# A transformer pair on one core: the first third rebuilt, with unnormed token-major products first and the depthwise convolution spread

## The reference, cut to what matters

```python
xn = rms_norm(h, norm1_g)                      # per token, then a gain per feature
proj = xn @ w_in                               # 1024 x 5136
sg_u, sg_v, g_q, g_k, g_v, g_r, g_a, a_q, a_k, a_v, c_a, c_g = split(proj)
y_a = gelu(sg_u) * (W_s layer_norm(gelu(sg_v)) + b)         # spatial gating, 128-token blocks
y_b = gated_linear_attention(g_q, g_k, g_v, g_r, g_a)       # 4 heads, chunks of 64
y_c = band_chunk_attention(a_q, a_k, a_v)                   # 8 heads, softmax
y_d = silu(layer_norm(causal_dwconv31(c_a * sigmoid(c_g))))  # 31 taps per channel
for n, y in enumerate((y_a, y_b, y_c, y_d)):
    merged += sigmoid(xn @ w_gate[n] + b_gate[n]) * (y @ w_branch[n])
h = h + merged @ w_out
h = h + relu(rms_norm(h) @ w_ff1)**2 @ w_ff2
h = h + sigmoid(rms_norm(h) @ w_ple_gate + b) * (p @ w_ple);  h = rms_norm(h)
```

## Time and profile before

| | us |
|---|---|
| three runs | 980.77, 983.38, 982.29; median 982.29 |
| the profiled execution | 980.21, of which the span 978.9 |
| TensorE busy, weight loads busy | 924.2, 892.8 |
| VectorE, ScalarE, GpSimd busy | 745.7, 551.5, 1.9 |
| HBM read | 186.53 MB, 192 GB/s over the span |

### The profile page before, as it was taken

One profiled execution on the slowest core, in us unless ns is written; L12 is line 12 of the kernel. 1 busy time (PEld: TensorE's weight loads), 2 busy tenths in 40 slices (PEclk: granted clock), 3 DMA queues, 4 the chain that ended last, 5 costly groups with the idle time before them and its releaser, 6 DMA issues.

```text
span 978.9 us, 18386 instructions
## 1 busy us (share of the span) xinstructions
PE 924.2 (94%) x7342; PEld 892.8 (91%) x7342; DVE 745.7 (76%) x1199; ACT 551.5 (56%) x789; POOL 1.9 (0%) x9
## 2 busy tenths in 40 slices
PE   5999998999999999999999779999999989999995
PEld 5998987899999999999999779989989989999995
DVE  6899989677566799988887789987667885555543
ACT  6565445667644676654444458658584564444442
POOL 0000000000000000000000000000000000000000
PEclk9999999999999999999999999999999999999998
DMA  6765534454464699988883345445344545555541
GB/s 241 230 186 207 162 126 151 130 194 149 154 208 134 211 346 331 393 315 319 314 301 115 111 158 172 151 148 157 128 132 154 187 154 193 196 196 192 183 141 44
DMA packets 52820, 188.77 MB, mean 193 GB/s; under 512 B 6000, under 2 KB 6784, under 8 KB 52608
## 3 DMA queue, kind: packets, MB, share of 16 engines
q1 hardware_dynamic: 52736, 187.60, 56.9%
HBM read 186.53 MB, written 1.05 MB: 192 GB/s over the span
## 4 chain that ended last, share of the span: by engine, by line
PE 64%; DVE 24%; ACT 7%; issue 4%; DMA 1%; SPq 0%; DVEq 0%; ACTq 0%
PE bank L867 20%; PE bank L870 19%; PE bank L869 19%; DVE wlo L900 8%; DVE cv L973 3%; ACT whi L1679 1%; DVE mqk L1250 1%; DVE nrm L915 1%; DVE scr L1084 1%; DVE t L948 1%; DVE Alo L941 1%; ACT L1687 0%; DMA araw<-in_ada 0%; DMA raw<-in_stream 0%; PE bank L608 0%
## 5 line engine op out<-in xcount | busy, mean ns | idle before, releaser
L900 DVE TENSOR_TENSOR wlo<-raw,whi 128x1024 fp32r<-128x1024 f32 x297 | 358.1, 1221 | 56.9 <-ACT whi L1679 56.4
L867 PE MATMUL bank<-Alo,whi 128*128 128x256 f32 x1312 | 373.1, 284 | 13.4 <-DVE wlo L900 9.0
L1679 ACT ACTIVATE whi<-raw 128x1024 fp32r<-128x1024 f32 x297 | 308.6, 1053 | 122.8 <-PE bank L870 112.5
L869 PE MATMUL bank<-Ahi,wlo 128*128 128x256 f32 x1312 | 367.2, 280 | 0.0
L870 PE MATMUL bank<-Ahi,whi 128*128 128x256 f32 x1312 | 366.8, 280 | 0.0
L867 PEld LDWEIGHTS bank<-Alo,whi 128*128 128x128 f32 x1312 | 247.3, 188 | 19.8 <-issue 17.5
L869 PEld LDWEIGHTS bank<-Ahi,wlo 128*128 128x128 f32 x1312 | 247.4, 189 | 0.7 <-issue 0.2
L870 PEld LDWEIGHTS bank<-Ahi,whi 128*128 128x128 f32 x1312 | 247.4, 189 | 0.0
L867 PE MATMUL bank<-Ylo,whi 128*128 128x256 f32 x256 | 76.1, 297 | 12.5 <-DVE wlo L1644 5.7
L870 PE MATMUL bank<-Fhi,whi 128*128 128x256 f32 (+1 forms) x288 | 81.5, 283 | 0.0
L869 PE MATMUL bank<-Fhi,wlo 128*128 128x256 f32 (+1 forms) x288 | 80.8, 281 | 0.0
(11 more groups left out here) (369 smaller groups left out, 1405.5 us busy)
## 6 DMA issues: line engine op xcount, KB each, us to landing
raw<-in_stream SPq DMA_DIRECT2D x297, 512.0 KB, 4.3
araw<-in_ada SPq DMA_DIRECT2D x48, 512.0 KB, 6.4
TB<-in_TB SPq DMA_DIRECT2D x1, 1536.0 KB, 7.4
H<-in_xT SPq DMA_DIRECT2D x4, 256.0 KB, 4.3
out<-H SPq DMA_DIRECT2D x4, 256.0 KB, 2.2
bc<-in_bc SPq DMA_DIRECT2D x1, 896.0 KB, 6.0
raw<-in_stream SPq DMA_DIRECT2D x4, 128.0 KB, 3.3
mats<-in_mats SPq DMA_DIRECT2D x1, 449.0 KB, 7.6
```

The costliest lines, as they stand in the source:

```text
L867: pe.matmul(os[j], wh, xl, start=k == 0 and (wide or j == 0), stop=False, skip_group_check=not wide)
L869: pe.matmul(os[j], wl, xh, start=False, stop=False, skip_group_check=not wide)
L900: v.tensor_tensor(wlo[:, s % NHL, :], raw[:, s % NRAW, :], whi[:, s % NHL, :].bitcast(F32), ALU.subtract).then_inc(*lo_v.up(s))
L1679: a.activation(whi[:, s % NHL, :], raw[:, s % NRAW, :], ACT.Copy).then_inc(*hi.up(s))
```

## The change

- **Order.** The plan starts with v, gv, gk (token-major), then cg, ca, ga, u, gq, gr, aq, ak, av. The branches come as 0, 1, 2, 3 (before 0, 1, 3, 2), and their operand buffers are exchanged to match. v, gv and gk use the unnormed operand; a token is a partition of their output, so the norm is a per-partition scale in ScalarE's drain (`rows`, and the gelu of v, which also accumulates the sum for the mean). cg's drain is the sigmoid alone, ca's one multiplication.
- **First product.** v has a loop of its own, which uses a slab's high half before it waits for the low half.
- **Loads.** ScalarE's queue issues the gain columns and x tiles 2, 3; SP issues x tiles 0, 1, slab 0 in two halves, slab 1, the rest of x, slab 2, the other columns, slabs 3 and 4, mats, slabs 5 and 6.
- **Splits of x.** The first one is an ACT copy with scale and one VectorE subtraction (`scaled_low`); `gain` and `ahead` are made alike.
- **Norm.** Squares go to four buffers and three additions of 512; task r1 sums per token (a column) and per row.
- **Side tasks** have their own steps for each engine, bare yields are gone, and the taps go to slab 71.
- **Parts before pairs.** VectorE makes the low part of a slab before the work of the pair that ends at that slab; ScalarE makes the high part first in the products of `AFTER_VECTOR`. The lows of the last branch (br3) follow one pair later.

```diff
+    t("w_in", (0,), 512, 512, 8)
+    t("w_in", (0,), 1536, 512, 8)
+    t("w_in", (0,), 1280, 256, 8)
     f("w_in", (0,), 4624, 4, 8)
     f("w_in", (0,), 4112, 4, 8)
...
+AFTER_VECTOR = ("br3", "wo", "ff2", "pg", "pm", "wo2", "dn") + tuple(f"zu{j}" for j in range(1, NF2 // 2))
+ASIDE = {("gv", 1): 4}
...
-    "xa": [4, 5, 6, 7, 7],
-    "conv": [*range(8, 47), 48, 49, 50, 51],
-    "sg": [12, 13, 14, 15, 16, 17, 19, 20],
-    "gla": [19, 20, 21, 22, 24, 25, 26, 27, 29, 32, 33, 36],
-    "att": [n for h in range(4) for n in (53 + 5 * h, 54 + 5 * h, 56 + 5 * h)] + [73],
+    "r1": ([3], [4], [3, 5]),
+    "xa": ([], [5, 6, 7, 8, 9], [5, 6, 7, 8]),
+    "sg": ([14, 14], [8, 11, 12, 15, 16, 22, 24, 25, 26], [9, 23, 24]),
+    "gla": ([19, 25, 28, 30, 32, 32, 34, 39], [20, 22, 24, 27, 29, 31, 36, 38, 41, 43],
+            [20, 21, 22, 25, 33, 34, 37, 39, 42]),
+    "att": ([n for h in range(4) for n in (44 + 6 * h, 48 + 6 * h, 50 + 6 * h)],
+            [n for h in range(4) for n in (45 + 6 * h, 47 + 6 * h, 51 + 6 * h)],
+            [n for h in range(4) for n in (45 + 6 * h, 48 + 6 * h, 50 + 6 * h)]),
+    "conv": ([73, 77], [*(n for n in range(18, 72) if n not in (36, 41, 63, 64)), 75, 79, 80, 81, 82, 83],
+             [73, 75, 77, 79, 80, 81, 82]),
-TAPS = [3] * 32 + [5] * 5 + [3]
+TAPS = [3] * 24 + [2] * 26
...
+                for k in range(K):
...
+                    w.wait_ge(*xh_s.at(k))
+                    w.wait_ge(*(hi.at(s) if s else hi.at("half", k)))
+                    for tt in range(2):
+                        pe.matmul(bs[tt][:, 0:m], xh[:, ts[tt]], wh, start=k == 0, stop=False)
+                    w.wait_ge(*xh_v.at(k))
+                    for tt in range(2):
+                        pe.matmul(bs[tt][:, 0:m], xl[:, ts[tt]], wh, start=False, stop=False)
+                    w.wait_ge(*(lo_v.at(s) if s else lo_v.at("half", k)))
...
+            def scaled_low(k, g, hi_, lo_, tile=None):
...
+                return v.scalar_tensor_tensor(out=lo_[:, k, 0:T], in0=H[:, k if tile is None else tile, :], scalar=g,
+                                              in1=hi_[:, k, 0:T].bitcast(F32), op0=ALU.mult, op1=ALU.subtract)
...
+                        if (name, n) in ENDS and ENDS[name, n] >= 1:
+                            low_part(ENDS[name, n] + 3)
                         after_pair(name, n, main[name, n])
...
+            a.dma_start(cols[:, 0:8], A["cols"][:, 0:8]).then_inc(*g1_in.up("in", by=16))
+            a.dma_start(H[:, 2:4, :], A["xT"][:, 2:4, :]).then_inc(*x_in[1].up("in", by=16))
+            w.wait_ge(*g1_in.at("in"))
+            for q in range(2):
+                first_high(q)
+                c = slice(q * 512, q * 512 + 512)
+                w.wait_ge(*first_in[q].at("in"))
+                a.activation(whi[:, 0, c], raw[:, 0, c], ACT.Copy).then_inc(*hi.up(("half", q), (q - 1,)))
+            for s in range(1, 4):
+                first_high(2 * s)
+                first_high(2 * s + 1)
+                high_part(s)
+            for p, t in enumerate((t512[0][:, :], t512[1][:, :], scr[:, 0:512], scr[:, 512:1024])):
+                square("r1", p, t)
```

More of the change, by code:

```diff
@@ L75, with main_banks @@
 WIDE = ("mq0", "zg0", "zu0")
+UNNORMED = ("v", "gv", "gk")
+AFTER_VECTOR = ("br3", "wo", "ff2", "pg", "pm", "wo2", "dn") + tuple(f"zu{j}" for j in range(1, NF2 // 2))
+ASIDE = {("gv", 1): 4}
+def main_banks():
+    out, n = {}, 0
+    for name, (kind, w, lead, c0, m, K) in zip(NAMES, plan()):
+        for p in range(2 if kind == "T" else -(-m // 2)):
+            if (name, p) in ASIDE:
+                out[name, p] = ASIDE[name, p]
+            else:
+                out[name, p] = n % 3
+                n += 1
+    return out
 LIMIT = {("w_in", 2560): 2576, ("w_in_2", 2048): 2056}
@@ L200, in build @@
     NS = n_slabs()
-    EVENTS = events()
-    steps = {}
+    EVENTS, ENDS = events(), slab_ends()
+    steps = [{}, {}, {}]
     for name, after in STEPS.items():
-        for n in after:
-            steps.setdefault(n, []).append(name)
+        for of, each in zip(steps, after if isinstance(after, tuple) else (after,) * 3):
+            for n in each:
+                of.setdefault(n, []).append(name)
+    pe_steps, v_steps, s_steps = steps
     with ctx:
@@ L351, in build @@
         raw_in = signals(" ".join(f"raw{i}" for i in range(NRAW)))
-        first_in = signals(" ".join(f"first{i}" for i in range(4)))
+        first_in = signals("first0 first1")
         x_in = signals("x0 x1 x2 x3")
@@ L391, in low @@
             return lo_v.at(s)
+        main = {of: banks[n] for of, n in main_banks().items()}
         def drained(name, p):
@@ L452, in sync_program @@
                             load_slab(int(s))
-                    for task in steps.get(n, ()):
+                    for task in v_steps.get(n, ()):
                         if task in tasks:
@@ L488, in sg @@
             def sg():
-                for _ in range(6):
-                    yield
                 for gp in range(2):
@@ L509, in gla @@
                 i.then_inc(*gla_pe.up("z"))
-                for _ in range(4):
-                    yield
+                yield
                 w.wait_ge(*mats_in.at("in"))
@@ L550, in gla @@
                     yield
+                for hf in range(2):
                     if hf:
@@ L892, in vector_program @@
             w = Waiting(v)
+            lows = set()
             def low_part(s):
-                if s >= NS:
+                if s >= NS or s in lows:
                     return
+                lows.add(s)
                 w.wait_ge(*hi.at(s))
@@ L1093, in gla @@
                                                ).then_inc(*gla_v.up("w", h))
+                    yield
+                    for pr in range(2):
+                        h = 2 * pr + hf
                         w.wait_ge(*gla_s.at("hi", h))
@@ L1701, in split_shifted, with r1 @@
                         yield
+            def r1():
+                w.wait_ge(*cols_in.at("in"))
+                w.wait_ge(*summed.at("r1c"))
+                a.activation(stat[:, 8:10], banks[5][:, 0:2], ACT.Sqrt, scale=1.0 / D, bias=col("eps")
+                             ).then_inc(*root.up("r1c"))
+                square_root("r1", 3)
+                yield
+                for p in range(2):
+                    w.wait_ge(*rstd.at("r1c"))
+                    w.wait_ge(*mm.at("v", p))
+                    a.activation(vt[:, p, :], main["v", p][:, :], ACT.Gelu_apprx_tanh, scale=stat[:, 10 + p:11 + p],
+                                 accum_out=stat[:, p:p + 1]).then_inc(*drained_s.up(("v", p)))
+                yield
             def xa():
```

455 lines of the change are left out of this document (224 added, 231 removed).

## The result

| | before | after |
|---|---|---|
| runs, us | 980.77, 983.38, 982.29, 983.45 | 960.41, 956.71, 955.27, 954.98 |
| median | 982.84 | 955.99 |
| profiled execution, its span | 980.21, 978.9 | 960.41, 958.8 |

The ratio is 0.9739, with a 95% interval of 0.9705 to 0.9774: faster, 5 us under the forecast of 961 and inside its range. The execution that was profiled is the slowest of the four, 4.4 us above their median.

A forecast was written before the change was run, and what follows sets the result against it. TensorE's matmul floor of 2.80 us a slab bounded it, plus side matmuls and waits, mostly for VectorE, which paced slabs 17 to 40. 8.4 + 9.5 − 0.4 + 3.7 = 21.2 us off gave 961, range 954 to 970.

The forecast's parts named there:

- start, to slab 4: Before slab 4: stops vanish and the clock rises earlier, so slab 4 starts at 20.9 instead of 29.31; 8.4 us gained.
- middle, to the end of `wo`: Middle of the first third: VectorE's waits and slow clock shrink, 9.5 us gained, less 0.4 for the larger sum task.
- later products: Products after the first third: 2.0 us in pg, 0.7 in ff1, 1.0 in wo2 and after; 3.7 together, between 1 and 7.
- a first matmul at 6.1: At the start: TensorE's first matmul comes at 6.1 us, between 5.2 and 7.2.
- it rose after 3.5 us without a stop: Clock at the start: it rose so before, hence full speed at about 11 us, with 9.5 and 13 as ends.
- The second queue counted as nothing: Loads at the start: issuing from ScalarE too is worth at most about 0.9 us; the sum counts nothing for it.
- The norm fits beside slabs 4 to 10: Root and reciprocal beside slabs 4 to 6; ScalarE and VectorE each have 15 of 16.8 us of work, so both fit.
- Rival one: ScalarE is late around slabs 8 to 10, stalling gk and cg: 7.7 us less gained, 969; chance 0.12.
- VectorE drops from pacing to just below: Slabs 17 to 40: VectorE's work falls from 81.8 to 75.6 us against TensorE's 79.6; 2 us of waits left.
- 48 taps more cost nothing: Taps reaching slab 71 beside attention and gates add 20 us; VectorE has 73 of 79 us of work, costed at nothing.
- The step that failed: In pg, VectorE's low half ahead of the pair's work doesn't shorten the 8.5 us cycle, only moves which slab waits.
- ahead's shorter tail: In pg, from H's addition to Alo takes 1.45 instead of 1.95 us on VectorE; four pairs, 2.0 us.

The follow-up runs named there:

- the table loaded early: Changed kernel with a one-column copy on ScalarE ahead of its wait for the gain columns, so its table loads sooner: 955.24 us against 955.99.
- the dense taps: Changed kernel with all convolution taps done by about slab 43, five a slab from slab 18, instead of spread to slab 71: 973.77 us, 17.8 slower.
- the filler: Changed kernel with one more VectorE operation of 384 columns, its result unread, behind the low half of each of slabs 44 to 71: 964.45 us, 8.5 slower.

## Why the prediction was right, and where it was wrong

The total came out for partly wrong reasons, and partly by luck. The profiled execution has the spell at 115 and another at 691. With the table loaded early, which otherwise does the same work, the profile has neither, though its spell behind 540 is 10.3 us long and not 6.8, and a span of 953.3. Read by it, the terms are:

| | forecast | profile after | without the two spells |
|---|---|---|---|
| start, to slab 4 | 8.4 | 7.1 | 7.8 |
| middle, to the end of `wo` | 9.5 − 0.4 | 7.3 | 10.4 |
| later products | 3.7 | 5.7 | 7.4 |
| sum, in the span | 21.2 | 20.1 | 25.6 |

- **The start** failed only in "a first matmul at 6.1": 6.97, within its bounds. I had weighed a table load ahead of the issues, not behind the wait. That transfers would be there in time, that no stop would come before slab 4, and full speed between 9.5 and 13 (12.2) all held. The reason given for the last, "it rose after 3.5 us without a stop", is weaker than it sounds: in the same trace TensorE ran without a stop from 8.65 to 12.8 and the clock did not rise, and in the profiles with the new start it rose 3.1 to 6.2 us after the first matmul. The sum task took 1.6 us instead of 1.0.
- **The second queue counted as nothing**: shown, with one queue no later. The Trainium skill (DMA: Bandwidth & Descriptors, "Issuing engines are not separate DMA queues") grants a second issuing engine only the time at the sequencer; by these runs even that doesn't reach the first matmul (6.36 us with one queue, 6.97 with two).
- **The norm fits beside slabs 4 to 10**: no wait for ScalarE before `gk` or `cg`; `cg` begins at 39.4. The drain that the Trainium skill (ScalarE: Activation LUTs, "What ACT_TABLE_LOAD costs") adds to a switch of sets does not show here: after the load at 21.28 in the table-early run the root starts at 22.58, 1.30 later, and in the changed kernel's trace the next instruction follows 28 of the 45 loads within 0.02 us. Rival one fell.
- **VectorE drops from pacing to just below**: shown from both sides, by the dense taps (17.8 us) and by the kernel before with the order alone, half of whose start's gain was eaten there. I left 2 us of waits between slab 17 and 40; there are 0.2. That and the 10.4 of the table put this term about 1 us too low.
- **"48 taps more cost nothing"**: held, with 1.5 us at the attention. But the cover was told by sums of busy time, and the filler shows that it ends some 4 us before they say.
- **The step that failed** is "the low half placed ahead of the pair's work doesn't shorten that cycle; it only moves which slab waits". The first half is true: with the order undone a cycle still takes 7.98 us. The second is not. The order is worth 7 us alone and 8.9 in the changed kernel, of which 4.7 and some 5 lie behind `wo`, where the term for everything was 3.7 and the table shows 7.4. The mistake was to look at `pg` alone, where VectorE is the bound and most of what the order saves in one stop comes back in the next. In `ff1` (VectorE busy for 81 of 90 us), `ple` and the attention, and at the first norm, VectorE has time to spare, and there the order decides who uses it: the weights, which TensorE meets at every slab, or a result that has two slabs in hand.
- **ahead's shorter tail**, 2.0 us in `pg`: right, 8.0 against 8.5 a cycle. The 0.7 for `ff1` was gained, but by the order.

In the profiled execution the errors partly cancelled (20.1 against 21.2), by the chance of its slow spells, which hid what the order brought; in the median they did not, and 26.9 us were gained.

The start can be taken apart further. Of the 4.4 us that came with the order alone, 2.9 are a stop and 1.5 slow clock. The changed kernel is at slab 4 another 2.8 us earlier: 2.8 of stops and 1.8 of slow clock are gone as well, less 1.3 for its later first matmul and 0.6 for its larger sum task. What stays open is which part of the new start removes those stops (the product on the unnormed operand, the matmuls of 512 columns, the loads), and how much of the clock is phase, since slab 4 begins anywhere from 21.5 to 22.95 in kernels with the same start.

## What to carry to other kernels

Where an engine serves a stream that the bound engine meets at every step and also does irregular work, put the stream's piece first in its order, except where the bound engine's very next operand is that irregular result; test the order by itself, since no sum of busy times showed its worth here. An early start is kept only if the next stretch isn't paced by another engine. And read a prediction's terms against an execution without chance spells of the slow clock, or a wrong term hides in them.

## What was not expected of the hardware

- ScalarE's first table load can end up behind a wait for data or ahead of it: at 4.50 us behind the first transfers in the changed kernel (3.89 with one queue), at 0.73 in the kernel before, whose first copy waited until 4.32 all the same, and at 1.65 once an instruction whose input was there at once stood ahead. No run here shows what decides between the two.
- TensorE fell to 1.2 GHz with no stop of its own, during and after a piece of 64-column matmuls, in four of nine profiles with the same piece, once for 6.8 us and three times for 3.4. It went with the time at which the clock had first risen (12.2 us or later against 11.0 or earlier), and that time does not follow the first matmul: 10.6 with a first matmul at 7.53, 12.2 with one at 6.97. So up to 3.4 us come and go between like kernels.
